# Constant products in TensorE's waits: the start, the last attention units, the first chunk's inverse, the group norm and the first layer norm

## What is computed

```python
for i in range(DEPTH):
    if i % 2 == 0: y = sliding_window_attention(h, ...)
    else:          y = rwkv7_time_mix(h, ...)       # ends in a norm per head, then y @ w_o
    h = layer_norm(ALPHA * h + y, ln_mix_g[i], ln_mix_b[i])
    y = swiglu(h, ...) if i % 2 == 0 else moe_swiglu(h, ...)
    h = layer_norm(ALPHA * h + y, ln_ffn_g[i], ln_ffn_b[i])
return h[:, N_META:]
```

## Time and profile before

| | us |
|---|---|
| median of 3 runs | 1576.52 |
| the three runs | 1575.29, 1576.52, 1577.91 |
| profiled execution, first to last instruction | 1579.1 |
| PE busy in it | 1531.7 (97%) |
| DVE, ACT, POOL busy | 525.0, 340.4, 125.6 |

### The profile page before, as it was taken

How to read it: one execution, slowest core, us unless ns; L and a number is a source line. 1 busy time by engine, 2 the same in 40 slices (tenths; PEclk the granted TensorE clock), 3 DMA queues, 4 the chain that set the end, 5 groups by cost and what they waited for, 6 DMA issues and landing times.

```text
span 1579.1 us, 42675 instructions
## 1 busy us (share of the span) xinstructions
PE 1531.7 (97%) x19642; PEld 1008.7 (64%) x19642; DVE 525.0 (33%) x858; ACT 340.4 (22%) x639; POOL 125.6 (8%) x148
## 2 busy tenths in 40 slices
PE   8999999999999998999999999999999999999996
PEld 6778999977989998733634635535436436346344
DVE  4756555456855457501011111110210211111113
ACT  4655444334812223400000000100100100000001
POOL 3320000300005332000000000000000000000000
PEclk9989999999989999999999999999999999999998
DMA  9623545621410002489999999999999999999980
GB/s 264 230 98 120 183 164 182 240 98 65 150 49 4 4 4 105 193 345 408 406 381 409 405 386 399 401 396 401 387 408 400 385 409 402 385 411 403 384 344 29
DMA packets 39985, 427.83 MB, mean 271 GB/s; under 512 B 4711, under 2 KB 4823, under 8 KB 7432
## 3 DMA queue, kind: packets, MB, share of 16 engines
q1 hardware_dynamic: 37672, 417.56, 67.0%
q0 software_dynamic: 2144, 7.66, 1.9%
HBM read 423.85 MB, written 1.12 MB: 269 GB/s over the span
## 4 chain that ended last, share of the span: by engine, by line
PE 73%; DVE 2%; issue 1%; ACT 0%; POOL 0%; DVEq 0%
PE PS L1226 55%; PE PS L995 6%; PE PS L651 5%; PE PS L1014 1%; PE PS L1023 1%; PE PS L1166 1%; DVE arena L1644 1%; PE PS L690 1%; PE PS L1215 1%; DVE z L1644 0%; PE PS L1216 0%; PE PS L1112 0%; PE PS L925 0%; PE PS L975 0%; PE PS L1139 0%
## 5 line engine op out<-in xcount | busy, mean ns | idle before, releaser
L1226 PE MATMUL PS<-ring,x_all 128*32 128x448 f32 x3072 | 296.7, 539 | 0.7 <-issue 0.7
L1226 PE MATMUL PS<-arena,x_all 128*32 128x448 f32 x3072 | 291.6, 539 | 0.0
L1226 PEld LDWEIGHTS PS<-ring,x_all 128*32 128x32 f32 x3072 | 112.9, 110 | 173.8 <-issue 171.2
L1226 PEld LDWEIGHTS PS<-arena,x_all 128*32 128x32 f32 x3072 | 100.0, 110 | 188.7 <-issue 188.7
L1644 DVE TENSOR_TENSOR experts<-experts,PS 128x1344 f32<-128x1344 f32 (+1 forms) x33 | 49.9, 1512 | 452.1 <-PE PS L1226 243.7
L1644 DVE TENSOR_TENSOR w_lo<-ring,w_hi 128x2048 fp32r<-128x2048 f32 x55 | 127.3, 2315 | 86.3 <-PE PS L651 53.4
L1226 PE MATMUL PS<-arena,hid_T 128*32 128x256 f32 x2688 | 150.1, 379 | 0.0
L1226 PE MATMUL PS<-ring,hid_T 128*32 128x256 f32 x2688 | 150.1, 379 | 0.0
L1320 ACT ACTIVATE w_hi<-ring 128x2048 fp32r<-128x2048 f32 x53 | 101.5, 1915 | 149.0 <-issue 83.9
L1226 PEld LDWEIGHTS PS<-ring,hid_T 128*32 128x32 f32 x2688 | 98.8, 110 | 50.6 <-issue 3.9
L1226 PEld LDWEIGHTS PS<-arena,hid_T 128*32 128x32 f32 x2688 | 102.1, 110 | 44.0
(11 more groups left out here) (295 smaller groups left out, 1766.5 us busy)
## 6 DMA issues: line engine op xcount, KB each, us to landing
ring<-in_moe SPq DMA_DIRECT2D x96, 1792.0 KB, 9.2
arena<-in_moe SPq DMA_DIRECT2D x96, 1792.0 KB, 9.4
ring<-in_slabs SPq DMA_DIRECT2D x58, 1024.0 KB, 4.9
arena<-in_lora POOLq DMA_DIRECT2D x1, 1152.0 KB, 5.4
h<-in_h SPq DMA_DIRECT2D x2, 544.0 KB, 5.4
arena<-bias_lines POOLq DMA_DIRECT2D x1, 1056.0 KB, 20.8
arena<-bias_lines POOLq DMA_DIRECT2D x1, 1040.0 KB, 25.9
ring<-in_slabs SPq DMA_DIRECT2D x4, 256.0 KB, 7.4
```

Of the source, the lines that this page charges most:

```text
L1226: mm = pe.matmul(out(j, b), x(b), piece, start=first(b), stop=last, skip_group_check=True)
```

## The change

A tile `idle` of 128 x 256 (in the place of the transposed probabilities, not yet used then) is set to 1.0 by DVE as its first instruction. PE waits for it, makes four products of it before the bias lines and eight behind them, where three of the one-hot table stood. `keep_clock` gets a place (`at`) and a form that neither clears nor closes a sum (`start=False`). Added are: two products of the identity per unit in units 18 to 23, into columns 384 to 511 of bank 7; six behind the first layer norm's broadcast; two behind each of the three levels of the first chunk; in the group norm one behind each of the first seven groups of sums (bank 0, columns 384 to 511), four behind the last, and eight behind the broadcasts. Nothing is removed but the three products of the one-hot table, and nothing else is moved. The semaphore `s_idle` is new.

```diff
+        idle = carve(14236, 256)
...
-            def keep_clock(n, bank):
+            def keep_clock(n, bank, at=0, start=True):
 
                 for _ in range(n):
-                    mm = pe.matmul(PS[:, bank, 0:P], same_head[:, :], ones_d[:, :], start=True, stop=True)
+                    mm = pe.matmul(PS[:, bank, at:at + P], same_head[:, :], ones_d[:, :], start=start, stop=start,
+                                   skip_group_check=not start)
                 return mm
...
-                if l == 1:
-                    keep_clock(12, 3)
-
-
+                if l < 2:
+                    keep_clock(12 if l else 6, 3)
+
+
+            def warm_up(n):
+
+                for _ in range(n):
+                    pe.matmul(PS[:, 7, 0:256], idle[:, 0:P], idle[:, :], start=True, stop=True)
+
+            pe.wait_ge(s_idle, 1)
+            warm_up(4)
             pe.wait_ge(s_attn, 32)
             for i in range(3):
                 n = min(512, 2 * LINE - 512 * i)
                 pe.matmul(PS[0:HEADS, i, 0:n], rbias[0:33, :], onehot[0:33, 512 * i:512 * i + n],
                           start=True, stop=True).then_inc(s_line_ps, 1)
-            for i in range(3):
-                pe.matmul(PS[:, 7, 0:256], onehot[0:33, 0:P], onehot[0:33, 0:256], start=True, stop=True)
+            warm_up(8)
             pe.wait_ge(s_line, 3)
...
                     elif r == 4:
                         pe.wait_ge(slab_taken, SL_WO + 1)
                         first_out(range(4), low=True)
+                    for _ in range(2):
+                        pe.matmul(PS[:, 7, 384:512], eye[:, :], eye[:, :], start=False, stop=False, skip_group_check=True)
...
                     for j in range(4):
                         mm = pe.matmul(PS[32 * j:32 * j + 32, 0, 0:CH], to_head[:, m, :],
                                        by_group(sq[:, m, TEXT])[:, j, :], start=m == 0, stop=m == KC - 1)
+                    if m < KC - 1:
+                        keep_clock(1, 0, 384, False)
                 mm.then_inc(gn_pe, 1)
+                keep_clock(4, 1)
                 pe.wait_ge(gn_dve, GN_ROOT)
...
                     mm.then_inc(gn_pe, 1)
+                keep_clock(8, 3)
...
                     levels = levels + 1
+                    if c == 0:
+                        keep_clock(2, 7)
...
+            dve.memset(idle[:, :], 1.0).then_inc(s_idle, 1)
             for i in range(3):
                 n = min(512, 2 * LINE - 512 * i)
                 dve.wait_ge(s_line_ps, i + 1)
```

More of the change, by code:

```diff
@@ L412, in build @@
         s_bias = [sem(f"bias{t}_loaded") for t in range(len(Q_TILES))]
-        s_ones = sem("ones_row_set")
+        s_ones, s_idle = sem("ones_row_set"), sem("idle_tile_set")
         qkv_kept = sem("qkv_kept")
```

## The result

The kernel with the change takes 1584.49 us, the median of six runs (1582.79 to 1586.95); the kernel before, run beside it, 1576.66 (six runs, 1575.29 to 1580.91). The ratio is 1.0052 with an interval of 1.0039 to 1.0065: slower by 7.8 us, 6.2 to 10.2. The prediction, 1575.9 in a range of 1571.8 to 1580.6, was wrong.

What follows compares the result with a forecast made beforehand. PE is busy 97% of the span, but in some slow-clock stretches DVE sets the pace. Start +1.7, attention +0.9, layer norm 0, inverse -0.5, group norm -1.5: 0.6 faster, 1575.9 us, range 1571.8 to 1580.6.

Steps and rivals of the forecast that it cites:

- -1.5: Group norm: seven products between the sums, 0.22 us each, push the last sum and the broadcasts 1.5 us later.
- the end of -2.8: Group norm: the worst end of the forecast, the seven products at 0.40 us each, 2.8 us lost.
- +1.7: Start: the first slab's 19 products run at the full clock, a gain of 1.7 us; ends +2.1 and -3.
- some 3.6 us of dense work raise the clock: Start: the four products before the bias lines raise the clock, so the eight end before the first rounded weights.
- rival (b): Start: the eight products delay the first slab at the low clock, -3 instead of +1.7; 1580.6 us, chance 0.11.
- the second step: Start: with bias lines 1.2 us earlier, unit 4's bias-table gate allows 2.1 us, so the 1.7 gain passes.
- 1.3 forecast: Last attention units: twelve added products cost 12 x 0.22 = 2.6 us, half of it hidden, leaving 1.3 lost.
- The saving of 2.2: Last attention units: a shorter slow stretch saves 1.7 to 2.7 of DVE's 4.3 us of waits, taken as 2.2.
- rival (d): Attention: the timed runs lack the falls, so nothing is saved; 1.6 us slower, 1578.1 us, chance 0.17.
- -0.5: First chunk's inverse: three pairs delay the levels by 0.5 us and the fall stays; ends +1.8 and -2.4.
- 0 was right: First layer norm: six products fit PE's idle 1.88 us and DVE sets the pace, so 0 gained or lost.

Runs made afterwards that it cites:

- The block ahead of the sums: Kernel before with the seven group-norm products as one block ahead of the first group of sums: 1578.61 us, ratio 1.0018.
- the start alone: Kernel before with only the idle tile, four products ahead of the bias lines and eight behind: 1574.46 us, ratio 0.9999.
- the covered products: Kernel before with only six products behind the first layer norm's broadcast, four and eight in the group norm: 1577.66 us, ratio 1.0008.
- The second execution of the kernel before: The kernel before with no edit, run for a second profile: 1577.03 us.

## Why the prediction was wrong

**Group norm, the term that was most mis-sized:** -1.5 was 7 x 0.22, the price of a product in a row of its like. The place was right (nothing hides them, root and broadcasts are later by the same time) and the forecast sign too; in alternation with the sums the seven cost 3.6 us, beyond the end of -2.8. The block ahead of the sums, 0.24 each, shows that the price depends on the neighbours. The 56 ns of the Trainium skill (TensorE: Matmul & The Clock Gate, section Back-to-back issue gap), which that section gives for an isolated gap beside 81 ns in a stream of weight loads and products, are further off: the measured 0.24 and 0.52 decide.

**Start:** +1.7 failed at the step "some 3.6 us of dense work raise the clock". In the change and in the start alone four products of 3.78 us did not; the bias lines were slow and rival (b) held, with a first slab 3.3 to 3.7 us late. Its -3 was too large, though: 1.2 are left at unit 4, whose time lies between 43.9 and 47.6 in the profiles with the old start, and twelve runs of the start alone show no loss. In the one profile where the clock did rise early, the second step failed: the last bias table landed no earlier, though 2.1 us had been allowed, and took the whole gain.

**Attention:** the price was right where there is no fall, 1.13 us (1.3 forecast); beside a fall it is 2.2. The saving of 2.2 failed: it was read off the fall of one execution, as rival (d) said. Of the eight profiles without pairs two have that fall, four have one of half its length and two have none. Alone the twelve cost 2.0 to 2.5 us.

**First chunk's inverse:** -0.5 agrees with the 0.5 measured, which is within the spread, and the fall stays as forecast. **First layer norm and the covered products:** 0 was right, in duration and in cover; the falls that vanished there gave nothing, DVE having no gap.

**What no term had:** in the change the clock fell in the third norm's ten products, 1.6 us. The second execution of the kernel before has the same 11.16, so it is not the change's alone.

**The sum:** -3.6 for the group norm, -1.2 at the start, -1.1 for the pairs and -0.5 for the inverse give 6.4 of 7.8 us. The parts alone (start 0, attention 2.5, the seven 4.1, inverse 1.6, covered products 1.3 slower) add up to 9.5, each with 2 us or so to either side; both agree with the measured 6.2 to 10.2. Why executions of one kernel differ in their falls, and which of them the change shifts, stays open.

**The range** ended at rival (b) and took the rivals one at a time. Rivals (b) and (d) both came true, (d) as far as the pairs saved nothing: together, at the prediction's own prices, they make it 3 + 1.3 + 0.5 + 1.5 = 6.3 us slower, 1582.8, outside the range before any term is put right.

The base was off too: the span was held against the median of times, without the 1.84 us around it. So the execution lay 4.4 us above the median, not 2.6, which would have spoken more strongly for rival (d). Its mean granted clock, 0.981, is the lowest that the 110 runs show.

## What to carry to other kernels

Before filling waits to hold a clock, ask of every slow stretch which engine is waited for, and read more than one execution: a fall that other profiles lack is no gain to count on, and falls also vary with nothing changed. Price a filler product where it will stand, among products of another shape, and put it in one block where a wait covers it, not one by one between the products that the next engine waits for. A higher mean clock is not a shorter time: here 27.5 us at the low level, where two profiles of the kernel before had some 48 and 34, came with 7.8 us more.

## What was not expected of the hardware

A 128 x 128 x 128 product took 0.24 us in a block and 0.52 between groups of sums of a 32-column shape, both at the full clock. The same six products of the bias lines, behind the same four of 3.5 to 3.8 us, took 3.80 us in one kernel's execution and 2.00 in another's, though the two programs are the same up to there, so that the moment of the first rise is no property of the program alone. The last bias table landed anywhere from 42.9 to 47.6 us after issues that lay 0.6 us apart. And executions of the unchanged kernel lay between 1572.1 and 1583.0 us, at mean granted clocks of 0.989 to 0.981, with two profiles of it that differ by a fall of 13.6 us.
